# A step of attention cut in two on the tensor engine: transposes and the next scores first, products with v behind another stage

## The reference

```python
def trunk_layer(x, m, lp, s_rwkv, s_ret, k_ctx, v_ctx, is_ctx):
    h = rmsnorm(x, lp['norm_mix_pre']) * (1.0 + sc1) + sh1
    z = h @ lp['w_in']
    out_a, st_rwkv = rwkv7_branch(z_rwkv, s_rwkv, lp)
    q, k, v = (t.reshape(B, T, H_B, DH_B) for t in jnp.split(z_na, 3, axis=-1))
    if is_ctx:
        o_na = dense_attention(q, k_ctx, v_ctx)
    else:
        o_na = neighbourhood_attention(q, k, v, k_ctx, v_ctx, lp['na_rpb'])
    out_b = o_na.reshape(B, T, D_B) @ lp['w_o_na']
    out_c, st_ret = retention_branch(z_ret, s_ret, lp, not is_ctx)
    merged = gates[:, :, 0] * out_a + gates[:, :, 1] * out_b + gates[:, :, 2] * out_c
    x = x + g1 * rmsnorm(merged @ lp['w_out'], lp['norm_mix_post'])
    h2 = rmsnorm(x, lp['norm_ffn_pre']) * (1.0 + sc2) + sh2
    x = x + g2 * rmsnorm(conv_ffn(h2, lp['ffn_up'], lp['ffn_conv'], lp['ffn_down']), lp['norm_ffn_post'])

# attention of one block of 128 queries q, with keys k and values v
s = jnp.einsum('bqhd,bhkd->bhqk', q, k).astype(F32) * (D ** -0.5)   # + bias, sample only
p = jax.nn.softmax(s, axis=-1).astype(v.dtype)
o = jnp.einsum('bhqk,bhkd->bqhd', p, v)
```

## Time and profile before

| What | Value |
|---|---|
| Median of 3 runs | 2222.61 us (2218.12 to 2227.48) |
| The profiled execution | 2219.63 us, its span 2217.8 us |
| TensorE busy | 1983.9 us, 89% |
| VectorE, ScalarE, GpSimd busy | 45%, 42%, 40% |
| Mean granted TensorE clock | 0.955 |
| One pair | 122 to 127 us, eight of them |

### The profile page before, as it was taken

The page is one execution under the profiler, slowest core; times in us unless marked ns, Lnnn a source line. Parts: engine busy times, 40 slices in busy tenths (PEclk is TensorE's granted clock), DMA queues, the critical chain, the costliest instruction groups (busy, mean ns, idle before and its releaser), DMA issues. The chain is left out here.

```text
span 2217.8 us, 42009 instructions
## 1 busy us (share of the span) xinstructions
PE 1983.9 (89%) x17656; PEld 1763.9 (80%) x17656; DVE 1006.3 (45%) x1492; ACT 935.9 (42%) x1744; POOL 879.0 (40%) x466
## 2 busy tenths in 40 slices
PE   4889899998999969999649898989999998899994
PEld 0877778787899959999608777777878997799994
DVE  2554646565531256560115546464756222465501
ACT  2643534354433354443236435453544334544431
POOL 0523416061355525555205233250604554355551
PEclk9899999999999989999878999999999999999997
DMA  7314223131433313333153141322314332233331
GB/s 275 120 33 129 65 96 98 60 116 40 146 116 126 115 54 125 125 125 120 39 213 122 41 134 50 114 80 80 104 49 142 127 124 96 72 127 124 125 114 48
DMA packets 64998, 233.23 MB, mean 105 GB/s; under 512 B 7328, under 2 KB 11680, under 8 KB 63904
## 3 DMA queue, kind: packets, MB, share of 16 engines
q1 hardware_dynamic: 58464, 215.21, 29.2%
q10 hardware_dynamic: 6336, 15.24, 1.9%
HBM read 223.58 MB, written 6.84 MB: 104 GB/s over the span
## 5 line engine op out<-in xcount | busy, mean ns | idle before, releaser
L1579 POOL TENSOR_TENSOR ringlo<-ring,whi 128x1024 fp32r<-128x1024 f32 x304 | 741.6, 2441 | 784.6 <-ACT whi L859 784.3
L436 PE MATMUL psz<-hhi,whi 128*128 128x386 f32 x1760 | 617.6, 351 | 44.4 <-DVE hlo L1229 44.4
L436 PE MATMUL psz<-hlo,whi 128*128 128x386 f32 x1760 | 606.2, 344 | 0.0
L436 PE MATMUL psz<-hhi,ringlo 128*128 128x386 f32 x1760 | 604.9, 344 | 0.0
L436 PEld LDWEIGHTS psw<-work 64*64 64x64 f32 (+2 forms) x9024 | 331.0, 140 | 97.1 <-issue 65.2
L436 PE MATMUL psw<-work 64*64 64x64 f32 (+3 forms) x9024 | 384.5, 235 | 23.1 <-ACT work L859 16.4
L436 PEld LDWEIGHTS psz<-hhi,whi 128*128 128x128 f32 x1760 | 339.1, 193 | 61.0 <-issue 43.9
L859 ACT ACTIVATE whi<-ring 128x1024 fp32r<-128x1024 f32 x304 | 320.3, 1054 | 141.2 <-PE psz L436 134.1
L436 PE MATMUL psz<-part,whi 128*128 128x386 f32 x1344 | 353.4, 344 | 2.8 <-DVE part L1229 2.8
L436 PEld LDWEIGHTS psz<-hlo,whi 128*128 128x128 f32 x1760 | 341.1, 194 | 2.1
L436 PEld LDWEIGHTS psz<-hhi,ringlo 128*128 128x128 f32 x1760 | 338.3, 192 | 0.0
(11 more groups left out here) (97 smaller groups left out, 1584.1 us busy)
## 6 DMA issues: line engine op xcount, KB each, us to landing
ring<-in_w SPq DMA_DIRECT2D x400, 512.0 KB, 3.4
pk<-in_pk ACTq DMA_DIRECT2D x8, 832.0 KB, 4.6
out_x<-work ACTq DMA_DIRECT2D x2, 1544.0 KB, 8.6
work<-out_x ACTq DMA_DIRECT2D x2, 1544.0 KB, 6.9
const<-in_const SPq DMA_DIRECT2D x1, 1923.0 KB, 7.6
work<-in_x SPq DMA_DIRECT2D x1, 1544.0 KB, 10.3
out_x<-work SPq DMA_DIRECT2D x1, 1544.0 KB, 5.1
out_nak<-work ACTq DMA_DIRECT2D x8, 64.0 KB, 3.2
```

What stands on the lines that cost most here:

```text
L436: ins = nc.tensor.matmul(out, a, b, start=start, stop=stop, skip_group_check=True)
L1579: L.do(G.tensor_tensor(out, a, b, op), S[sig] if sig else None)
```

## The change

`attend(i)` on TensorE no longer has the products with v. It has the transposes of job i-2 (`flip_mm`) and the scores of job i. The products with v (`values_mm`) stand by themselves, one stage later. On ScalarE the step is cut in three: copies of the transposes and the scores (`attend`), the exponential (`powers`) and the copy of v's result (`values`).

The places change too. Steps 1 and 2 stand in the middle of the tenth and eleventh projections instead of ahead of the tenth and between the two. Step 3 moves behind the `am` products, step 4 to level 1, and so on, so that each later step stands one stage later. In a level the products with v stand behind the second 24 products. In level 4 two `ada_steps` move behind them, and so does the transpose of retention's keys (`keys_flipped`). On GpSimd the `low` of block `sb_ + 8`, the tenth projection's, moves behind the copies to `pend` and the product `rr` of the second direction. What is computed stays the same.

```diff
-                    def dense(zi, j, src=hsp, wait=None):
+                    def dense(zi, j, src=hsp, wait=None, between=None):
                         for k in range(KT):
+                            if between and k == KT // 2:
+                                between()
...
                         def attend(i):
                             if i >= 2:
-                                values_mm(i - 2)
+                                flip_mm(i - 2)
                             if i < 6:
                                 scores_mm(i)
+                        def keys_flipped():
+                            pe.wait_ge(*at_of("no_ready", p, 5))
+                            tr(w(5, 0, P), tk[:, 0:P], "kt_done")
...
-                        attend(1)
-                        dense(zb + 10, bb + 8)
-                        attend(2)
-                        dense(zb + 11, bb + 9)
+                        dense(zb + 10, bb + 8, between=lambda: attend(1))
+                        dense(zb + 11, bb + 9, between=lambda: attend(2))
                         turned(zb + 12, zb + 10, mixed[2][p])
-                        attend(3)
+                        values_mm(0)
...
+                            if lv <= 4:
+                                attend(lv + 3)
                             if lv == 1:
-                                attend(5)
...
                                 retain(lv - 4)
-                                ada_steps(2)
+                                if lv == LEVELS - 1:
+                                    ada_steps(2)
...
+                            if lv <= 4:
+                                values_mm(lv + 1)
+                            if lv == 4:
+                                ada_steps(2)
+                                keys_flipped()
```

ScalarE, which in the lines ahead of a pair's levels has `powers(i)` behind `attend(i)` for the first three steps, and `values(0)` behind the copy of the last projection:

```diff
+                        powers(3)
+                        values(1)
                         for lv in range(1, LEVELS):
                             run(gg.rearrange("p h x c -> p h (x c)"), psw[:, b:b + 2, 0:384], sig="gl_ready")
+                            if lv <= 4:
+                                attend(lv + 3)
...
+                            if lv <= 4:
+                                powers(lv + 3)
+                                values(lv + 1)
+                            if lv == 4:
+                                retain(0)
```

VectorE's steps move one place later with the others, its `attend(3)` to behind the transpose that gives `x_ready`. GpSimd:

```diff
-                            low(sb_ + 7 + d)
+                            if d == 0:
+                                low(sb_ + 7)
...
-                        low(sb_ + 9)
+                        for j in (sb_ + 8, sb_ + 9):
+                            low(j)
```

More of the change, by code:

```diff
@@ L550, in scores_mm, with flip_mm @@
                                 mm(w(4, P, 256), q, nk[rows(hb), LAT:TP], sig="sc_done")
-                        def values_mm(j):
-                            hb, kind = JOBS[j]
-                            n = 3 if kind else 1
+                        def flip_mm(j):
+                            n = 3 if JOBS[j][1] else 1
                             pe.wait_ge(*at_of("pn_ready", p, j))
@@ L559, in values_mm @@
                                 tr(w(5, i * P, P), scores[j % 2][:, i * P:(i + 1) * P], "pt_done" if i == n - 1 else None)
+                        def values_mm(j):
+                            hb, kind = JOBS[j]
+                            n = 3 if kind else 1
                             pe.wait_ge(*at_of("pt_ready", p, j))
@@ L579, in retain @@
                                 pe.wait_ge(*at_of("s_ready", p, 5))
-                                pe.wait_ge(*at_of("no_ready", p, 5))
                                 freed(zb + 7)
@@ L584, in retain @@
                                 mm(w(4, 256, 256), perm, tk[:, LAT:TP], sig="rope_done")
-                                tr(w(5, 0, P), tk[:, 0:P], "kt_done")
                             elif i in (1, 2):
@@ L667, in _ @@
                                                sig="am_done" if (x % 2, k, c) == (1, 1, 1) else None)
-                        attend(4)
+                        attend(3)
                         for hb in range(2):
@@ L674, in _ @@
                                        vt[hc(c), x % 3, rows(hb)], sig="g0_done" if (x, c) == (5, 1) else None)
+                        values_mm(1)
                         for lv in range(1, LEVELS):
@@ L689, in _ @@
                                 d = lv - 2
-                                attend(lv + 4)
                                 pe.wait_ge(*at_of("bkp_ready", p, d))
@@ L996, in attend @@
                             if i >= 2:
[L997 to L1000, removed]
+                                n = 3 if JOBS[i - 2][1] else 1
+                                act.wait_ge(*at_of("pt_done", p, i - 2))
                                 run(ptr[:, 0:n, :], w(5, 0, n * P).rearrange("p (k q) -> p k q", k=n), sig="pt_ready")
-                                act.wait_ge(*at_of("no_done", p, j))
-                                run(mixed[1][p][rows(hb), TT[kind]:TT[kind] + P], psw[rows(hb), 5, 3 * P:4 * P], sig="no_ready")
                             if i < 6:
@@ L1006, in attend, with values, powers @@
                                 run(scores[i % 2][:, 0:P], w(4, 0, P), sig="sctx_ready")
+                        def values(j):
+                            hb, kind = JOBS[j]
+                            act.wait_ge(*at_of("no_done", p, j))
+                            run(mixed[1][p][rows(hb), TT[kind]:TT[kind] + P], psw[rows(hb), 5, 3 * P:4 * P], sig="no_ready")
+                        def powers(i):
+                            if i < 6:
                                 act.wait_ge(*at_of("mx_ready", p, i))
@@ L1057, in _ @@
                         attend(0)
+                        powers(0)
                         seen(zb + 9)
@@ L1060, in _ @@
                         attend(1)
+                        powers(1)
                         seen(zb + 10)
@@ L1063, in _ @@
                         attend(2)
+                        powers(2)
                         seen(zb + 11)
@@ L1067, in _ @@
                         run(tv, z(zb + 12, 384).rearrange("p (t c) -> p t c", t=3), free=zb + 12)
-                        attend(3)
+                        values(0)
                         for d in range(2):
@@ L1105, in _ @@
                                                 scale=lg[:, i:i + 1])
-                            else:
-                                retain(lv - 4)
+                            if lv <= 4:
[3 more added lines that the diff above has]
+                                retain(0)
                         for hb in range(2):
@@ L1451, in retain @@
                                 stt(tk, w(4), -1.0 / 64, tq, op1=ALU.add, sig="ryc_ready")
-                        for i in range(4):
+                        for i in range(3):
                             attend(i)
@@ L1469, in _ @@
                         flip(xv, tvv, "x_ready")
-                        attend(4)
+                        attend(3)
                         for lv in range(1, LEVELS):
                             if lv < 4:
-                                attend(4 + lv)
+                                attend(3 + lv)
                             else:
```

## The result

| Kernel | Median, us | Ratio to the kernel before | 95% interval |
|---|---|---|---|
| before | 2221.58 (4 runs) | | |
| changed | 2164.91 (4 runs) | 0.9743 | 0.9721 to 0.9765 |

The change saves 57 us; 45 were forecast, 2178, in a range of 2158 to 2198. The profiled execution took 2164.02 us, 55.6 less than that of before.

A forecast was written before the change was run, and what follows sets the result against it. TensorE, busy 89%, bounds the kernel through its waits and half clock. Eight pairs at -4.9 us give -39, half clock -9 and +3: together -45, 2174.6 us, plus 3.0 for the runs' median, 2177.6; range 2158 to 2198.

The forecast's parts named there:

- The waits behind the transposes: TensorE's six waits a pair for ScalarE's copy of the transposes all go: -4.96 us a pair.
- The masks of the levels: Products with v, moved ahead of the next level's first products, cover the wait for VectorE's mask in four levels: -1.0 us.
- the transposes' ends: Idle time counted from the transposes' modelled end misses about 0.2 us for each of six: -1.2 us a pair.
- the first level: After the am products, TensorE waits 0.5 us for x_ready and 0.5 for ScalarE's copy ahead of job 2's transposes: +1.0 us.
- The tenth projection: Its weights come later from GpSimd, so its start stays while the scores now lie behind; gap 3.3 us: +0.8 us a pair.
- A pair at full clock: The local terms sum to -5.2 us a pair; -4.9 taken for unseen waits, -39 in eight pairs.
- The half clock in level 1: The half-clock stretch behind the 1.42 us wait goes in seven pairs, 1.31 us each: -9 us.
- The half clock behind the tenth projection: The gap grows, so the half-clock stretch behind it stays in seven pairs and comes to the eighth: +3 us.
- Rival 3: The half-clock stretch at the tenth projection goes, since the projection that follows is one dense block: 2154 us; chance 11%.
- the first: Rival: the second half-clock stretch, in level 1, stays or moves: 2187 us; chance 23%.
- the fourth: Rival: slower, the clock stays at half from the tenth projection through the am products and levels: 2272 us; chance 4%.
- The second: Rival: VectorE and ScalarE become the levels' chain, late by 0.6 us in four levels: 2197 us; chance 15%.

The follow-up runs named there:

- e6: e1, but in levels 1 to 4 the products with v stand ahead of the second 24 products instead of behind them; 2145.9 us, ratio 0.9664.
- e1: The changed kernel with GpSimd's old order, the tenth projection's block made ahead of the copies to pend and rr; 2139.7 us, ratio 0.9649.
- e2: The kernel before with only GpSimd's move of the tenth projection's block behind the copies and rr; 2249.0 us, ratio 1.0139.
- e3: The kernel before with steps 1 and 2 inside the tenth and eleventh projections, not cut, GpSimd as before; 2202.1 us, ratio 0.9927.
- e5: The kernel before with ten more TensorE products, whose result nobody reads, at the start of every pair; 2232.2 us, ratio 1.0052.
- e4: e1 with steps 1 and 2 back at the projections' borders: the cut and the new places behind the projections alone; 2160.6 us, ratio 0.9741.
- e8: e1 run once more, unchanged, as the measure for runs beside it; 2139.8 us, ratio 0.9637.

## Why the prediction was right, and where it was not

**The waits behind the transposes** (-4.96 us a pair): right, all six went. The group fell to 9.3 us, where the forecast named some 15.

**The masks of the levels** (-1.0): too large, e6 measured 0.47. The pieces of -1.2 for the transposes' ends and +1.0 for the first level weren't measured apart. In the first level the wait for x_ready was 0.32 where 0.5 was put, and the one for ScalarE's copy ahead of job 2's transposes doesn't show at all.

**The tenth projection** (+0.8, bounds 0.5 and 1.3): its size came out by luck, from two errors that cancel. The step read GpSimd's two copies and rr as 2.24 us, from rows of before in which they stood beside VectorE's products. In the new order they took 1.58 (1305.78 to 1307.36), so TensorE started 8.18 us behind the turned values instead of 9.0, and that gave back the 0.8. The gap of 2.50 stands at the prediction's own sign that GpSimd's part is wrong (shorter than 2.5). What the step did not follow was VectorE: its last two products fell behind both blocks, the maximum of job 0 came 3.2 us later, and step 1 waited 0.84 us for it, which put the 0.8 back. The stretch at full clock kept its length, 19.87 as against 19.84, with the wait of 0.64 in step 2 and the product with v gone from it. The passage on the shared port pair had the mechanism at hand and drew it the wrong way: the danger was not that VectorE would hold GpSimd up, but that GpSimd, with two blocks in a row, would hold VectorE up. e1 and e2 show its price, some 25 and 30 us.

**A pair at full clock**: -4.1 measured, -4.9 taken. That is 7 us of 39 too many, and the masks account for 4 of them. Where the other 3 went was not tested.

**The half clock in level 1** (-9): right. All seven stretches went with the wait of 1.42 us. The kernels that keep that wait (before, e2, e3, e5) have a stretch there in 28 of 32 pairs; the eight that cut the step have none in 64.

**The half clock behind the tenth projection** (+3): this step failed. It took the gap's length to decide, so that a longer gap would keep the 6.8 us stretch in seven pairs and bring it to the eighth. Measured from the stretches around the projection: in before the seven cost 20 us over full clock, after the six cost 0.6 each, 4 in all, partly because half of their loss lies under the wait for VectorE. So this term was -16 and not +3. Rival 3 named the place, with 11%; its reason was the dense projection behind the gap. By the reading of e5 the reason is another: the gap stayed, and the pairs, no longer 126.3 us long, no longer fell with it at the place where a stretch lasts 6.83 us. e4 bears this out, where the scores still stand behind the gap and no stretch is long; for the two of the changed kernel that begin ahead of the gap's end, the dense projection remains open. This one error, 19 us, less the 7 of the terms above, is the 12 between forecast and result. That the time fell within the range rests on the width of the range and on errors of opposite sign.

**The bounds**: the sum of the terms' lower bounds gives about 2165, as the prediction has it, but that of the upper ones gives about 2206 and not 2188.

The Trainium skill ("TensorE: Matmul & The Clock Gate", section on HAM oscillation) led the forecast to a low clock in every pair. The page tells it of waits of some 3 to 5 us, longer than the 2.5 here, and the trace doesn't agree for the changed kernel: two of its eight pairs have none. The page also says, in the section on what is actually happening, that the point of transition varies with where the work falls, and e5 agrees: equal work and equal gaps of 2.5 us gave 3.41 us in four pairs and 6.83 in two.

**The rivals**: the first did not come, since no pair has half clock in its levels, nor did the fourth. The second did not come either. VectorE's steps in levels 1 and 2 ended in time, and the only wait for it there is the 0.32 for x_ready ahead of level 1, which was in the forecast.

## What to carry to other kernels

When a step has a hand-over to another engine in its middle, cut it there and put the halves one stage apart; here the cut alone gave 59 us, 12 of them by the clock behind an unchanged gap, against 57 for the whole change, whose other two parts nearly cancelled each other. When an instruction is moved past others on an engine, look at who runs beside its new place, not only at who waits for it: two GpSimd blocks back to back made VectorE's products, 1.0 us before, last 5.4. And when stretches at half clock repeat alike from one turn of a loop to the next, price them as a spread, not as a constant, since any change of the turn's length can move them.

## What the runs showed of the hardware

- A gap of 2.5 us on TensorE was followed by no stretch at half clock (1.2 GHz), one of 3.41 us or one of 6.83 us, with the same instructions before and behind it within each kernel: in before none once and 6.83 five times, in e5 3.41 four times and 6.83 twice, in e4 none three times and 3.41 three times. With gaps of 1.00 us (e1, e8, six pairs each) none fell there.
- The longer stretches all began ahead of the gap's end or at it, with one exception (e6, 1.2 us behind a gap of 1.97); those that began over 0.2 us behind it were otherwise 3.41 us. With gaps of 5.6 to 6.6 us (e2) they were 6.83 in seven pairs and 10.24 in one.
- Two VectorE products with both inputs in SBUF took 1.02 us beside small copies of GpSimd (before, e1), and 5.31 to 5.37 beside two of its 128x1024 subtractions in a row (e2, the changed kernel). The Trainium skill ("SBUF — State Buffer", section on SBUF's two separate sides) has VectorE and GpSimd lock their shared port pair for a whole instruction; the trace agrees. The first product, begun inside GpSimd's first block (1307.74), took 2.69 us and ended 0.4 us behind that block; the second ended 0.4 us behind the second block (1312.69 and 1313.11), so that one product got through per block.
